# Attention steps of a two-layer hybrid decoder on one core: value products ahead of the transposes in TensorE's program

## The reference, cut to what matters

```python
(q_n, kc, vc, ksl, vsl, kwn, vwn, g_n, q_d, k_d, v_d, g_m) = jnp.split(u @ w_in, offs, axis=-1)
y_nsa  = nsa_attention(...)  @ w_bn      # 8 query heads, 2 key/value heads, three branches
y_diff = diff_attention(...) @ w_bd      # 4 heads, each the difference of two softmaxes
g_a, g_b = jnp.split(jax.nn.sigmoid(g_m), 2, axis=-1)
return (g_a * y_nsa + g_b * y_diff) @ w_o
```

## Time and profile before

| | |
|---|---|
| median of 3 runs | 1617.99 us (1617.69 to 1618.09) |
| the profiled execution | 1617.69 us, span 1615.9 us from first to last instruction |
| granted TensorE clock, mean | 0.998 |
| TensorE products busy | 1591.8 us, 99% of the span |
| VectorE busy | 1027.2 us, 64% |
| ScalarE busy | 640.2 us, 40% |

### The profile page before, as it was taken

One profiled execution on the slowest core, in us unless ns is written; L12 is line 12 of the kernel. 1 busy time (PEld: TensorE's weight loads), 2 busy tenths in 40 slices (PEclk: granted clock), 3 DMA queues, 4 the chain that ended last, 5 costly groups with the idle time before them and its releaser, 6 DMA issues.

```text
span 1615.9 us, 21448 instructions
## 1 busy us (share of the span) xinstructions
PE 1591.8 (99%) x8418; PEld 1276.3 (79%) x8418; DVE 1027.2 (64%) x1602; ACT 640.2 (40%) x1144; POOL 83.4 (5%) x139
## 2 busy tenths in 40 slices
PE   7999999999999999999999999999999999999997
PEld 3878777778878888888888877777887888888886
DVE  4597787869885666667576767776668433333344
ACT  2542455455263332222265235545645433232221
POOL 2400000000010011010020000000000000000000
PEclk9999999999999999999999999999999999999999
DMA  9954222255346666665346321112332333334322
GB/s 310 310 163 135 59 61 66 66 157 167 94 120 193 206 189 188 186 209 173 91 142 183 91 66 53 40 40 92 91 91 79 105 92 104 95 101 123 96 86 75
DMA packets 277684, 201.48 MB, mean 125 GB/s; under 512 B 6904, under 2 KB 263216, under 8 KB 276816
## 3 DMA queue, kind: packets, MB, share of 16 engines
q1 hardware_dynamic: 264112, 147.95, 31.5%
q0 software_dynamic: 12608, 43.77, 8.9%
q10 hardware_dynamic: 864, 8.39, 1.3%
HBM read 193.79 MB, written 6.29 MB: 124 GB/s over the span
## 4 chain that ended last, share of the span: by engine, by line
PE 90%; DVE 5%; DMA 3%; ACT 1%; issue 1%; SPq 0%; DVEq 0%; ACTq 0%
PE banks L1762 23%; PE banks L1764 23%; PE banks L1763 23%; PE banks L1944 3%; PE banks L1972 2%; PE banks L1913 2%; DMA ada_first<-in_w_ada_dram 2%; PE banks L1919 1%; PE banks L1850 1%; PE banks L1849 1%; PE banks L1848 1%; PE banks L1923 1%; PE banks L1978 1%; DMA ring<-in_w_in_dram 1%; DVE w_lo L1105 1%; PE banks L1831 1%
## 5 line engine op out<-in xcount | busy, mean ns | idle before, releaser
L1762 PE MATMUL banks<-u_hi,w_hi 128*128 128x512 f32 x1112 | 450.0, 405 | 2.1 <-DVE u_lo L1357 2.1
L1105 DVE TENSOR_TENSOR w_lo<-ring,w_hi 128x1024 fp32r<-128x1024 f32 (+3 forms) x239 | 286.7, 1201 | 253.9 <-ACT w_hi L789 252.5
L1764 PE MATMUL banks<-u_hi,w_lo 128*128 128x512 f32 x1112 | 434.1, 390 | 0.0
L1763 PE MATMUL banks<-u_lo,w_hi 128*128 128x512 f32 x1112 | 433.9, 390 | 0.0
L789 ACT ACTIVATE w_hi<-ring 128x1024 fp32r<-128x1024 f32 (+2 forms) x242 | 250.1, 1033 | 148.0 <-PE banks L1764 86.1
L1762 PEld LDWEIGHTS banks<-u_hi,w_hi 128*128 128x128 f32 x1112 | 209.2, 188 | 45.2 <-issue 5.0
L1764 PEld LDWEIGHTS banks<-u_hi,w_lo 128*128 128x128 f32 x1112 | 208.9, 188 | 44.7
L1763 PEld LDWEIGHTS banks<-u_lo,w_hi 128*128 128x128 f32 x1112 | 209.6, 189 | 36.3
L994 ACT ACTIVATE probs<-banks,neg_max 128x128 f32<-128x128 f32 (+3 forms) x192 | 99.0, 524 | 145.5 <-DVE neg_max L1564 145.5
L1763 PE MATMUL banks<-h_lo,w_hi 128*128 128x512 f32 x352 | 137.0, 389 | 0.0
L1764 PE MATMUL banks<-h_hi,w_lo 128*128 128x512 f32 x352 | 136.9, 389 | 0.0
(11 more groups left out here) (281 smaller groups left out, 2281.5 us busy)
## 6 DMA issues: line engine op xcount, KB each, us to landing
ring<-in_w_ffn_in_dram SPq DMA_DIRECT2D x88, 512.0 KB, 3.9
ada_ring<-in_w_ada_dram POOLq DMA_DIRECT2D x80, 512.0 KB, 4.3
ring<-in_w_in_dram SPq DMA_DIRECT2D x72, 512.0 KB, 3.8
ring<-in_w_ffn_out_dram SPq DMA_DIRECT2D x32, 448.0 KB, 3.4
ada_first<-in_w_ada_dram SPq DMA_DIRECT2D x16, 512.0 KB, 7.5
ring<-in_w_out_dram SPq DMA_DIRECT2D x16, 512.0 KB, 3.6
ring<-in_w_ffn_out_dram SPq DMA_DIRECT2D x16, 512.0 KB, 3.6
w<-in_cmp_w_k_dram SPq DMA_DIRECT2D x8, 512.0 KB, 6.8
```

Of the source, the lines that this page charges most:

```text
L1105: V.tensor_tensor(lo, src, hi.bitcast(fp32), ALU.subtract).then_inc(split_lo, 1)
L1762: M(bank, wh[:, block], sh[:, k, :], start=start, stop=False)
L1763: M(bank, wh[:, block], sl[:, k, :], start=False, stop=False)
L1764: return M(bank, wl[:, block], sh[:, k, :], start=False, stop=stop)
```

## The change

In TensorE's turn of the loop, the value products of step t-2 stand behind the first gate unit and ahead of the transposes of step t-1, instead of at the turn's end. Nothing is added or removed, no wait is changed, and no other engine's program is touched.

```diff
                     for m, k in units if t == STEPS else units[:1]:
                         merge_gate(l, m, k)
+                    if t >= 2:
+                        values(l, t - 2)
                     if 1 <= t <= STEPS:
                         turn(l, t - 1)
                     for m, k in () if t == STEPS else units[1:]:
                         merge_gate(l, m, k)
-                    if t >= 2:
-                        values(l, t - 2)
```

## The result

The changed kernel takes 1633.2 us (median of 4 runs, 1632.5 to 1633.4), the kernel before 1618.0. The ratio is 1.0093, interval 1.008 to 1.0105: slower by 15.2 us where 12.7 was forecast, inside the stated range. The profiled execution took 1633.14 us. The clock of TensorE stayed granted: 0.995 to 0.998 in the runs of either kernel.

A forecast was written before the change was run, and what follows sets the result against it. The prediction took TensorE's own issue to bound the kernel, with under 3 us of waiting inside attention. From 1617.7 us, 6.8 + 5.4 − 1.0 + 1.5 = +12.7 us gave 1630.4 us, range 1624 to 1634.5.

The forecast's parts named there:

- part 2: VectorE's copy and its queue come later behind later transposes, so scores wait longer: +5.4 us, bounds 0 to about +9.
- the rival of the dearer load: Transposes behind value products: loading weights costs as much as a gate product's; +9.2 in the shapes' term, 1632.2 us, chance 0.10.
- What bounds it: TensorE's own issue in attention; the order can win at most 3 us of waiting, each added switch is paid in full.
- Part 1, the order of shapes: 48 nsa value steps at +0.151 us each, less 0.47 where masks follow: +6.8 us.
- The pair that no row showed: Value products (128*64) to transposes (128*128): taken as 0.203 us, from value products to 128*128 masks, the nearest pair.
- The free switch: Rival: the transposes' weights load while the last value products run; +7.3 us in all, 1625.0 us, chance 0.11.
- the wait at step 13: Layer 0's scores at step 13, behind a turn with an extra VectorE item: TensorE waits 0.97 us instead of 0.12.
- The subtraction: Delays carried through all 40 steps of both layers, each item with its duration and order: +3.0 us layer 0, +2.4 layer 1.
- the check of the method: Done for the order before, the same reckoning gives every turn's start within 0.6 us over a whole layer.
- Part 3: Nine waits for `mix` ahead of transposes are covered by the value products: −1.0 us.
- Part 4, the end of the layers: Turn 40: nothing covers ScalarE's copy between the last transposes and value products; TensorE idles 0.73 us more, twice: +1.5 us.
- The rival "VectorE becomes the bound": Hand-overs dearer by 0.15 us let delays run on between turns with extra items: waits +12 to +15, 1638 us, chance 0.10.

The follow-up runs named there:

- b_shape_only: Kernel before, with the value products put straight behind the transposes, which keep their place: 1625.97 us against 1618.05, ratio 1.0049.
- b_turn_later: Kernel before, with the transposes one gate unit later in each turn and the number of shape changes unchanged: 1623.62 us, ratio 1.0035.
- a_extras_first: Changed kernel, with VectorE's extra items of a turn ahead of the copy of the turned probabilities: 1624.84 us, ratio 1.004 against the kernel before.
- a_wide_only: Changed kernel, with values early only where they are 128*128 (cmp and diff), before turn 40; nsa values at the turn's end: 1621.29 us, ratio 1.0019.

## Why the prediction was right, and where it was short

The parts were right in kind and the sum was 2 us short, nearly all of it in part 2; the range owes nothing to errors that cancel between the parts. The total alone wouldn't have shown that: at 1633.2 us it is nearer to the rival of the dearer load (1632.2) than to the forecast (1630.4). The starts inside the turns decide between the two.

- **What bounds it.** Right: with at most 3 us of waiting to win in attention, one more switch a turn couldn't be repaid. The transposes' waits fell by 1.0 us, as forecast.
- **Part 1, the order of shapes**: forecast +6.8, measured +6.6. The pair that no row showed behaves as its nearest row: value products to transposes 0.203 to 0.204 apart by start (46 of 48; the two at step 5 are 0.24, a rest of the wait for `mix`), the first transpose 0.166 to the second where it was 0.109, lasting 0.329. The mean of L1944 rose from 273 to

```profile
L1944 PE MATMUL banks<-cst,probs 128*128 128x128 f32 x416 | 61.2, 279 | 0.0
```

  48 of 416 transposes with 56 ns more are those 6 ns. The free switch is out, and so is the gate product's load ahead of transposes: 0.057 was measured, not the 0.107 to which the figure of the Trainium skill (TensorE: Matmul & The Clock Gate, LDWEIGHTS) led. `b_shape_only` shows that the cost is the order's own, with VectorE in time.
- **Part 2, VectorE's lateness**: right in mechanism, too small: +5.4 forecast, +7.3 measured. (The growths listed for layer 0 add up to 3.1, not 3.0, and 219.80 later by 1.18 is 220.98, not 220.95; neither matters here.) `b_turn_later` makes the waits without an added switch, `a_extras_first` takes them away with TensorE's order kept. The size: in the chain from the earlier trace rows in the changed kernel,

```profile
217.21 1.21 DVE L1105 TENSOR_TENSOR w_lo<-ring,w_hi 128x1024 fp32r<-128x1024 f32 x1
...
218.34 0.17 DVE L1519 RECIPROCAL coef<-sums 128x4 f32<-128x4 f32 x1
...
218.55 1.38 DVE L1524 TENSOR_SCALAR probs<-probs,coef,gates 128x256 f32<-128x256 f32 x4
...
219.85 1.22 DVE L1564 TENSOR_REDUCE neg_max<-banks 128x4 f32<-128x1024 f32 x1
...
222.11 0.68 DVE L1594 TENSOR_TENSOR t<-q_raw 128x512 f32<-128x512 f32 x1
...
222.82 0.69 DVE L1595 TENSOR_REDUCE d_sq<-t 128x4 f32<-128x512 f32 x1
223.08 0.70 PE L1919 MATMUL banks<-kdT,qdT 64*128 64x256 f32 x4 [0.92 <-ACT probs L994]
223.54 0.17 DVE L1531 RECIPROCAL d_mix<-sums 128x2 f32<-128x2 f32 x1
```

  the wait at step 13 is 0.99 against 0.97 reckoned. What was too small is most likely the time that saving and squaring a tile's result take on VectorE. The subtraction, whose working is not printed, let each item of VectorE begin 0.08 us before the one ahead of it had ended, as independent items do (217.21 + 1.21 − 0.08 is the next start). Saving and squaring are items linked by a wait: 222.11 to 222.82 is 0.71 for one of 0.68, and the next follows at 223.54, again 0.03 behind the end. Two such hand-overs a turn, each 0.11 us dearer than assumed, come to 0.22 us, an estimate. Of the waits beyond the forecast, most lie two turns behind such turns, at steps for which it had 0.05 or less: 20 (0.38 in each layer), 31 (0.20 in each), 12 and 14 in layer 1 (0.27 and 0.18). Not all of it fits: step 6 waits 0.11 longer in each layer than forecast without such an item ahead of it, and step 13 of layer 1 waits 0.27 less, which is what step 12 had waited already. That the linked items are the cause is read from where the waits lie and is not shown; no run takes them away alone, for `a_extras_first` moves them with the rest. Nor could the check of the method have shown it: starts that agree within 0.6 us over a layer don't test single waits of 0.2 to 0.5.
- **Part 3**, the waits for `mix`: right, and only because each turn's own values cover `mix`; `a_wide_only` shows what happens without.
- **Part 4, the end of the layers**: forecast 1.5, measured 1.7 as a gap, and 1.2 to 1.3 as what its removal gives back. The 0.73 us a layer doesn't follow from the numbers beside it, for 1.06 − 0.11 − 0.06 is 0.89. Measured, the last transpose and the first value product are 0.96 apart, and that product takes 0.10 longer to the next one (0.21 where the others take 0.11).
- **The rival "VectorE becomes the bound"** didn't come about: the delays fade within two or three turns, because turns without extra items have room.

## What to carry to other kernels

When TensorE is the bound, look at the order of its work by array shape before moving anything: a group of 64-column or 64-row products between full-width neighbours pays at both ends, and moving it can add an end. A producer moved later in a turn costs what is queued behind its consumer, so the remedy may be a reordering on the consumer's engine: put work that is already possible ahead of the instruction that waits. When a pipeline is drained, look at the last turns by themselves; what covered a copy in the loop may not be there.

## What the runs showed of the hardware

The unexpected point is how constant a change of array shape is. Between starts it adds 0.09 to 0.10 us, whether the engine goes to 64 columns (gate product to value products 0.327, to transposes 0.231), to 64 rows (value products of `diff` to scores 0.205, to transposes 0.112), or back to the full array (value products of `nsa` to transposes 0.210 from the last pair, pair to pair 0.109). On top comes what of the next weights' load can't go ahead: 0.057 us for transposes (0.166 from the first to the second, where it is 0.109), 0.11 for a gate product (0.337 where it is 0.231), about 0.05 for 64 columns (0.153 where it is 0.102). The rows of the loads show it. In the kernel before, transposes behind a gate product have their first load with that product, 0.23 us ahead of the first transpose at 308.94; in the changed kernel, behind 128*64 value products, load and transpose start together:

```profile
308.71 1.03 PEld L1944 LDWEIGHTS banks<-cst,probs 128*128 128x128 f32 x8
```

```profile
215.47 0.86 PEld L1944 LDWEIGHTS banks<-cst,probs 128*128 128x128 f32 x8 [0.17 <-issue]
215.47 1.09 PE L1944 MATMUL banks<-cst,probs 128*128 128x128 f32 x8
```

The Trainium skill (TensorEngine Tiling (Array Packing), Key Properties) says that a change of tiling mode drains the engine; these runs agree, as far as starts can show it, and put the price at 0.10 us here.
